# A transformer backbone in two layers on one core: the post-norm gates reach all partitions by transfers through DRAM, and layer 1's conditioning adds up in four strips

## The reference, cut to what matters

```python
def ada_params(cvec, w, b):                       # w: (1024, 6 * 1024)
    return jnp.split(jax.nn.silu(cvec) @ w + b, 6, axis=-1)

def pre_mod(x, g, shift, scale):
    return rms_norm(x, g) * (1 + scale) + shift

def post_add(x, y, g, gate):
    return x + gate * rms_norm(y, g)

for l in range(DEPTH):                            # DEPTH = 2
    need_ctx = l < DEPTH - 1
    sh1, sc1, g1, sh2, sc2, g2 = [m[:, None, :] for m in ada_params(c, ada_w[l], ada_b[l])]
    csh1, csc1, cg1, csh2, csc2, cg2 = ada_params(c_ctx, ada_w[l], ada_b[l])
    ...
    x = post_add(x, y, mix_post_g[l], g1)
    f = conv_ffn(pre_mod(x, ffn_pre_g[l], sh2, sc2), ffn_w_up[l], ffn_conv_w[l], ffn_conv_b[l], ffn_w_down[l])
    x = post_add(x, f, ffn_post_g[l], g2)
    if need_ctx:
        ...                                       # the same for xc with cg1, csh2, csc2, cg2
```

## Time and profile before

| | |
|---|---|
| runs of the kernel before | median 1597.65 us (1597.47 to 1603.56, three runs) |
| the profiled execution | 1596.83 us, of it 1595.0 us span from the first to the last instruction |
| PE busy | 1487.5 us, 93% |
| DVE, ACT, POOL busy | 966.3, 722.4, 596.5 us |
| granted TensorE clock, mean | 0.979 of full speed |

### The profile page before, as it was taken

One profiled execution on the slowest core, in us unless ns is written; L12 is line 12 of the kernel. 1 busy time (PEld: TensorE's weight loads), 2 busy tenths in 40 slices (PEclk: granted clock), 3 DMA queues, 4 the chain that ended last, 5 costly groups with the idle time before them and its releaser, 6 DMA issues.

```text
span 1595.0 us, 22240 instructions
## 1 busy us (share of the span) xinstructions
PE 1487.5 (93%) x7628; PEld 1202.1 (75%) x7628; DVE 966.3 (61%) x1476; ACT 722.4 (45%) x1242; POOL 596.5 (37%) x529
## 2 busy tenths in 40 slices
PE   4988898999999999999999698899999999999997
PEld 1877467787888888887888576677777888888886
DVE  2457687557687668743334575788885544444455
ACT  2332476544332333223353545487775544444453
POOL 2351354242222222322333531375552344443454
PEclk8999899999999999999999899999999999999999
DMA  8230850112464346311222111110002233332232
GB/s 336 56 98 1 293 184 1 53 59 87 145 184 117 109 145 184 105 40 53 63 65 66 48 53 55 52 53 1 1 1 81 78 93 94 103 92 67 92 95 103
DMA packets 128122, 143.89 MB, mean 90 GB/s; under 512 B 7164, under 2 KB 95488, under 8 KB 127024
## 3 DMA queue, kind: packets, MB, share of 16 engines
q1 hardware_dynamic: 128048, 142.91, 28.6%
HBM read 140.79 MB, written 2.10 MB: 90 GB/s over the span
## 4 chain that ended last, share of the span: by engine, by line
PE 82%; DVE 7%; ACT 3%; DMA 3%; POOL 2%; issue 2%; SPq 0%; DVEq 0%; POOLq 0%; ACTq 0%
PE ps L470 23%; PE ps L471 22%; PE ps L472 22%; PE ps L1427 4%; PE ps L1413 3%; PE ps L1438 2%; DMA start_w<-in_ada_w_dram 2%; PE ps L1440 2%; DMA ada_w<-in_ada_w_dram 1%; PE ps L2075 1%; PE ps L1330 1%; POOL w_lo L462 1%; PE ps L924 1%; DVE hT_lo L803 1%; ACT prob L1467 1%
## 5 line engine op out<-in xcount | busy, mean ns | idle before, releaser
L462 POOL TENSOR_TENSOR w_lo<-raw,w_hi 128x1024 fp32r<-128x1024 f32 (+1 forms) x183 | 346.9, 1898 | 627.5 <-ACT w_hi L455 627.5
L470 PE MATMUL ps<-hT_hi,w_hi 128*128 128x512 f32 (+1 forms) x1096 | 387.5, 354 | 9.3 <-DVE hT_lo L803 5.0
L471 PE MATMUL ps<-hT_lo,w_hi 128*128 128x512 f32 (+1 forms) x1096 | 384.8, 351 | 0.0
L472 PE MATMUL ps<-hT_hi,w_lo 128*128 128x512 f32 (+1 forms) x1096 | 382.6, 349 | 0.0
L455 ACT ACTIVATE w_hi<-raw 128x1024 fp32r<-128x1024 f32 (+1 forms) x200 | 172.9, 866 | 197.0 <-PE ps L472 166.2
L470 PEld LDWEIGHTS ps<-hT_hi,w_hi 128*128 128x128 f32 x1096 | 207.1, 189 | 47.1 <-DVE hT_lo L803 6.0
L472 PEld LDWEIGHTS ps<-hT_hi,w_lo 128*128 128x128 f32 x1096 | 206.5, 188 | 28.8
L471 PEld LDWEIGHTS ps<-hT_lo,w_hi 128*128 128x128 f32 x1096 | 207.1, 189 | 26.9
L2301 DVE TENSOR_TENSOR g_lo<-act_g,g_hi 128x768 fp32r<-128x768 f32 (+1 forms) x82 | 104.2, 1277 | 155.9 <-ACT g_hi L2256 155.5
L470 PE MATMUL ps<-w_hi,g_hi 128*128 128x512 f32 x410 | 160.4, 391 | 3.5 <-DVE g_lo L2301 3.0
L472 PE MATMUL ps<-w_hi,g_lo 128*128 128x512 f32 x410 | 159.6, 389 | 0.0
(11 more groups left out here) (247 smaller groups left out, 2500.7 us busy)
## 6 DMA issues: line engine op xcount, KB each, us to landing
raw<-in_ffn_w_up_dram SPq DMA_DIRECT2D x84, 512.0 KB, 3.9
ada_w_up<-in_ada_w_dram SPq DMA_DIRECT2D x48, 512.0 KB, 4.2
raw<-in_ffn_w_down_dram SPq DMA_DIRECT2D x84, 256.0 KB, 2.6
ada_w<-in_ada_w_dram SPq DMA_DIRECT2D x32, 512.0 KB, 5.2
start_w<-in_ada_w_dram SPq DMA_DIRECT2D x8, 1024.0 KB, 11.4
raw<-in_c_w_qkv_dram SPq DMA_DIRECT2D x12, 512.0 KB, 3.7
raw<-in_ab_w_in_dram SPq DMA_DIRECT2D x8, 512.0 KB, 4.8
raw<-in_ab_w_out_dram SPq DMA_DIRECT2D x8, 512.0 KB, 4.3
```

The lines of the kernel that those rows point to most:

```text
L462: by.tensor_tensor(w_lo[:, slot, 0:width], raw[:, n % RAW, 0:width], w_hi[:, slot, 0:width].bitcast(F32), ALU.subtract).then_inc(lo_split, 1)
L470: nc.tensor.matmul(outp, s_hi, m_hi, start=first, stop=False, skip_group_check=True)
L471: nc.tensor.matmul(outp, s_hi, m_lo, start=False, stop=False, skip_group_check=True)
L472: return nc.tensor.matmul(outp, s_lo, m_hi, start=False, stop=last, skip_group_check=True)
```

## The change

The gate products and their copies go. SP writes the finished gate rows to an internal DRAM tensor once per layer (`gate_out`), and reads each gate back as one row to 128 partitions (`gate_in`), at the end of the out loads (layer 0), behind the fourth out load (layer 1), and at the end of the up loads (both layers). Layer 1's conditioning has other rows: stream v, half h of the columns at partition 64 v + 32 h, all in bank 6; so the sums have four strips, and bias, transposes, columns and gate gains follow in pieces of 512 columns.

```diff
-        select_v = keep("select_v", [P, 2, 32])
+        select_v = keep("select_v", [P, 32])
...
+        ada1_rows = beside_up[0][:, 0, 0:BANK]
...
-            return 96 + 2 * (5 - i) + v if l else 2 * i + v if i < 2 else 32 + 2 * (i - 2) + v
+            return 64 * v + 5 - i if l else 32 + 2 * (i - 2) + v
...
-        def ada_turn(pe, n, b):
+        def ada_rows_turn(pe, n, b):
 
             pe.wait_ge(s("ada_biased"), n)
-            for k in range(KC):
-                mm = nc.tensor.transpose(bank(b, 2 * BANK)[:, k * P:(k + 1) * P], gate_rows[:, k * P:(k + 1) * P],
-                                         ident[:, :])
+            for c in range(4):
+                mm = nc.tensor.transpose(bank(b)[:, c * P:(c + 1) * P], gate_rows[:, c * P:(c + 1) * P], ident[:, :])
             mm.then_inc(s("ada_turned"), 1)
...
+        def ada1_bias(dve):
+
+            dve.wait_ge(s("ada_rows_landed"), 16 * (2 + ADA1_SMALL))
+            for v in range(2):
+                for half in range(2):
+                    rows = slice(64 * v + 32 * half, 64 * v + 32 * half + 6)
+                    op = nc.vector.tensor_tensor(gate_rows[rows, 0:BANK], ada1_rows[rows, :], beside_up[2][rows, 0:BANK],
+                                                 ALU.add)
+            op.then_inc(s("ada_biased"), 1)
...
+        gate_copy = (nc.dram_tensor("gate_copy0", (8, D), F32, kind="Internal").ap(),
+                     nc.dram_tensor("gate_copy1", (2, D), F32, kind="Internal").ap())
+        GATE_COPIES = (1, 3)
+
+        def gate_out(sp, l):
+
+            sp.wait_ge(s(f"gates_made{l}"), 1)
+            if l == 0:
+                sp.dma_start(gate_copy[0][:, :], gate_rows[ADA0_ROW:ADA0_ROW + 8, :]).then_inc(s("gates_out"), 16)
+            else:
+                for sub in range(2):
+                    r = ada_row(1, (2, 5)[sub], 0)
+                    sp.dma_start(gate_copy[1][sub, :].rearrange("(h n) -> h n", n=BANK), gate_rows[r:r + 33:32, 0:BANK]
+                                 ).then_inc(s("gates_out"), 16)
+
+        def gate_in(sp, l, sub):
+
+            sp.wait_ge(s("gates_out"), 16 * GATE_COPIES[l])
+            for v in range(1 if l else 2):
+                row = sub if l else 6 * sub + v
+                sp.dma_start(gate[:, v, :], gate_copy[l][row, :].partition_broadcast(P)
+                             ).then_inc(s(f"{('mixpost', 'ffnpost')[sub]}{l}_gate"), 16)
...
-            dve.wait_ge(s(f"{tag}_gate"), 2 * (2 if nt == ALL_T else 1))
+            dve.wait_ge(s(f"{tag}_gate"), 16 * (2 if nt == ALL_T else 1))
...
+                if l == 1 and m == 3:
+                    sp.wait_ge(s("qk_steps1"), rope_plan(1)[0][-1])
+                    gate_in(sp, 1, 0)
+            if l == 0:
+                gate_out(sp, 0)
+                sp.wait_ge(s("mixpost0_acc"), ALL_T)
+                gate_in(sp, 0, 0)
...
-                    if l == 1 and n == 0 and k == 1:
-                        gates()
                     for j in TURN_BEHIND[l].get(k, ()) if last else ():
                         if j == 0:
-                            pe.wait_ge(s(f"{tag}_gate"), 4 if nt == ALL_T else 2)
+                            pe.wait_ge(s(f"o_read{l}"), 2 * len(groups))
+                            pe.wait_ge(s(f"o_sum{l}"), 2 * len(groups))
+                            pe.wait_ge(s(f"{tag}_ysq"), OUT_DONE[l])
                         mid_turn(pe, l, j)
-                if l == 0 and n == 1:
-                    gates()
...
+            if l == 0:
+                sp.wait_ge(s("ada_mac"), (TURNS - 1) * (2 * KC) + START_MACS)
+            else:
+                sp.wait_ge(s("mixpost1_post"), post_count(LAT_T, LAT_T - 1, 3, "mixpost1"))
+            gate_in(sp, l, 1)
...
             if l == 0:
-                for half in range(2):
-                    nc.tensor.matmul(ps[96:128, 6 + half, :], select[:, 0:32],
+                for r in range(0, P, 32):
+                    nc.tensor.matmul(ps[r:r + 32, 6, :], select[:, 0:32],
...
                 for v in range(ada_streams):
                     for half in range(2):
-                        mm = nc.tensor.matmul(ps[96:128, 6 + half, :], select_v[:, v, :],
+                        r = 64 * v + 32 * half
+                        mm = nc.tensor.matmul(ps[r:r + 32, 6, :], select_v[:, :],
                                               beside_up[0][:, v, half * BANK:(half + 1) * BANK],
                                               start=False, stop=True, skip_group_check=True)
...
-            gate_tensor(pe, l, tag, 1, (0, 1))
-
...
-                if half == 0 and nt == ALL_T:
-                    gate_tensor(pe, l, tag, 1, (2, 3))
                 if l == 0 and half == 1:
-                    pe.wait_ge(s(f"{tag}_gate"), 4)
-                    ada_turn(pe, 2, 6)
+                    ada_rows_turn(pe, 2, 6)
...
                 if l == 0:
+                    gate_out(sp, 1)
```

More of the change, by code:

```diff
@@ new lines, in ada1_columns @@
+        def ada1_columns(dve):
+            dve.wait_ge(s("ada_turned"), 2)
+            turned = bank(6).rearrange("p (c r) -> p r c", r=P)
+            for sub, v in ((0, 0), (0, 1), (1, 0)):
+                for half in range(2):
+                    kk = slice(4 * half, 4 * half + 4)
+                    r = 32 * half + ada_row(1, 3 * sub, v)
+                    g = 16 * sub + 8 + 4 * half
+                    nc.vector.tensor_copy(add_col[:, sub, v, kk], turned[:, r, :])
+                    nc.vector.scalar_tensor_tensor(out=mul_col[:, sub, v, kk], in0=turned[:, r - 1, :], scalar=1.0,
+                                                   in1=cols[:, g:g + 4], op0=ALU.add, op1=ALU.mult)
+            for half in range(2):
+                rows = slice(32 * half, 32 * half + 6)
+                op = nc.vector.tensor_tensor(gate_rows[rows, 0:BANK], gate_rows[rows, 0:BANK], beside_up[3][rows, 0:BANK],
+                                             ALU.mult)
+            op.then_inc(s("gates_made1"), 1)
@@ L700, in start_tensor @@
                         norm_turn(pe, "mix0", k)
-            pe.wait_ge(s("ada_biased"), 1)
-            for c in range(4):
-                mm = nc.tensor.transpose(bank(START_TURNED)[:, c * P:(c + 1) * P], gate_rows[:, c * P:(c + 1) * P],
-                                         ident[:, :])
-            mm.then_inc(s("ada_turned"), 1)
+            ada_rows_turn(pe, 1, START_TURNED)
             close(pe, "pe")
@@ L1765, in out_tensor @@
             batches = out_batches(l, nt)
-            def gates():
-                pe.wait_ge(s(f"o_read{l}"), 2 * len(groups))
-                pe.wait_ge(s(f"o_sum{l}"), 2 * len(groups))
-                pe.wait_ge(s(f"{tag}_ysq"), OUT_DONE[l])
-                gate_tensor(pe, l, tag, 0, range(4 if nt == ALL_T else 2))
             for n, batch in enumerate(batches):
@@ L1913, in out_scalar @@
             else:
-                gate_scalar(act, tag, range(2))
                 second_half(0)
```

85 lines of the change are left out of this document (22 added, 63 removed).

## The result

The changed kernel took 1578.8 us (median of 4 runs, 1576.78 to 1582.88) against 1597.56 us for the kernel before on the same chip, ratio 0.988 with an interval of 0.986 to 0.991: 14.7 to 22.4 us off. The forecast was 1579.2 us, 18.4 us off.

A forecast was written before the change was run, and what follows sets the result against it. The prediction took TensorE (PE), busy 93% of the span, as the bound. Gates 8.5 us plus strips and related 9.9 us made 18.4 us off 1597.65, giving 1579.2 us; range 1573 to 1589.

The forecast's parts named there:

- The gate products: Out and down projections of both layers: gate products leaving PE save 3.91 + 1.72 + 1.72 + 0.6 + 0.55 = 8.5 us.
- the inner pair: Layer 0's down, after its first three units: two gate products leave PE and their 1.72 us comes back whole.
- (d): Rival: granted clock falls to half at other moments, 1 to 2 us either way; only widens the range, no chance given.
- the sum: Whole kernel: gates 8.5 plus strips and related 9.9 give 18.4 us off, 1579.2 us; forecast as summed has 78%.
- the starts: Start of each down: unit 1 waits for g_lo anyway, so 0.6 and 0.55 us saved, not 1.98 each.
- The strips: Layer 1's conditioning in the up projection: sums save 5.1 and 3.6, zero product 0.8; with 0.4 from transposes, 9.9 us.
- What is added: Gate transfers on SP's queue and smaller DVE operations: price 0, bounded by 2 us; layer 0's out gates land near 314.
- The margin: Layer 0's out: gates landing at 314 against a need by about 317.4, 3.4 us to spare, 0.7 slack on top.
- a landing at 11.4 us: Layer 0's out: if the gate reads took 11.4 us, they would land at 319.3 and cost about 1.5 us.
- (a): Rival, layer 1's conditioning: strips do not overlap, 9.5 us of sums and zero products stay, 1588.7 us; 7%.
- (b): Rival: PE less free, chains over DVE, ACT, POOL end last in out projections, up meets DVE; half kept, 1588; 9%.
- (c): Rival, layer 0's out: one-row broadcast uses few engines; with one, 53.5 us transfer, gate 46 us late, 1625 us; 3%.

The follow-up runs named there:

- the two halves: Against the kernel before, each half of the change alone: gates by transfers only, 1587.76 us, ratio 0.9926; conditioning in four strips only, 1592.4 us, ratio 0.9952.

## Why the prediction was right

**What bounds the kernel.** That PE is the bound, and that what leaves it comes back, held: 9.3 us in a stage where PE was busy 344.89 of 345.

**The gate products.** 3.91 us in layer 0's out: 3.90 from the last product with `ow_ada` to the transposes, in both executions of the changed kernel. Over the whole stage it is 3.9 in the kernel with only the transfers, 3.5 in the changed one and 1.9 in its other execution; these losses lie ahead of the place where the products stood, and in the last case the granted clock was 0.91 in the 20 us before it (288 to 308). 1.72 us in the inner pair: shown by putting it back, 1.7. 1.72 in layer 1's out: 1.7 in one execution, 0.2 in the other, whose granted clock over the stage is 0.94 for 0.97. That isn't rare: of the eight executions with gates by transfers three have 59.2 us there with the clock at 0.94, and five 57.7 to 58.0 at 0.97, while none of the six with gates by products has 0.94. So in three of eight the clock took this term back, which rival (d) allowed for either way and the sum did not. 0.6 and 0.55 at the starts: 0.57 and 0.45, with the wait seen, and seen to go when products fill it. This was the step on which 2.8 us hung, between the slots and the distances, and the distances were right.

**The strips.** 9.5 us predicted in the up projection, 9.3 measured; the difference is the 0.98 of two strips for the 0.92 assumed, four times. The wrong step was to take half of a pair, 1.83 / 2, for the time of one product and so for the bound from below: a product alone takes 0.97. The Trainium skill's rule for a pack of column tiles (TensorE: Matmul & The Clock Gate, Measured speedup vs the span model) is one product's duration plus 4 ns for each further tile. With the 0.97 it gives, as an estimate, some 0.98 for two and for four, and the rows show 0.98 and 0.99. The rule holds here to 0.01 us, and the 0.90 to 0.92 that the prediction worked out from it had the wrong duration put in.

**What is added.** Price 0, and nothing was paid: PE never waited for a gate. The landing at 6.1 us behind the release (the sixth first-half tile done) was met (5.8 from the issue, which follows it at once). The margin was mis-sized, 3.4 us with 0.7 on top for 5.6: my reckoning amounts to 20.9 us from the first use to the transposes (339.0, which is 342.94 less 3.91, minus 318.1), the runs show 19.7, and the gates came 0.3 us sooner than I had them: 4.1 + 1.2 + 0.3 = 5.6. As I read the rows, the last tiles follow one another on DVE faster than on PE when the chain is pressed, which a reckoning back from one tile doesn't see; that reading wasn't tested by itself. The statement that a landing at 11.4 us costs 1.5 us was wrong with it; 5 us late cost nothing.

**The rivals.** (a) and (b) are excluded by the two halves. (c) was a fair rival with a good price: over one engine the gates come 36.4 us later than they do, 5.6 are covered, and PE waits 30.55. It was 11 us too dear in the transfer, since one engine moved 1.04 MB in 42.2 us, 24.7 GB/s with the issue and the landing in it, and not at the 19.6 that I had from the mean of the whole queue. (d) was sized too small for a single execution: the way to layer 0's attention alone, which no edit touches, takes from 230.3 to 236.0 us in the changed kernel.

**The sum.** By the stages that the change touches it is 3.5 + 9.3 + 2.6 + 1.7 + 0.3 = 17.4 us in the changed kernel's first profile, for 18.4. By the medians it is 18.8 and 22.9. The difference is layer 1's projection, 1.3 to 5.3 us shorter, of which 0.9 us goes with the faster load, part with the clock, and the rest has no shown cause, less 0.4 to 1.5 us that layer 1's attention gives back, and the way to layer 0's attention, which spreads over 3.7 us in three executions of the kernel before and 5.7 in two of the changed one. So 1579.2 was close to the first median partly by luck, because two small misses of opposite sign met: about 1 us too much for the touched stages, and a gain outside them that the prediction didn't have.

## What to carry to other kernels

Price a removed instruction by the distance to the next thing that must wait anyway, and not by its slot: the same pair of products was worth 1.72 us inside a stage and 0.5 at its start. Small sums that write one strip of the array belong side by side in one bank; beyond the first strip they are nearly free. Don't take half of a pair for the time of one: a row of one alone was in the trace. A broadcast through DRAM takes some 5 us for 512 KB, 5.8 to the first use for two of them, and apart from SP's issues no engine's time, so put it where its first use is that far behind its release, and read all 128 partitions in one transfer: split as 127 and 1, two of them took 42.2 us.

## What the runs showed of the hardware that I had not expected

One, two and four fp32 products in strips of their own cost the same, 0.97, 0.98 and 0.99 us, for 1.83 and 3.55 of two and four in one strip. A transfer over one engine ran at 24.7 GB/s and held the issuing queue: SP's four issues took 27.11 us, and the weight loads behind them waited. A load of one size in one place takes 3.6 or 4.9 us until it is used, the same within 0.1 us in the three executions of before and in the two of the changed kernel, and different between kernels, by a cause that I didn't find. And a wait of 5.25 us on PE cost 6.8 us in all: over the 8 us from 345.00 on, the wait's last 0.4 and what follows, the granted clock was 0.70, more than half of them at the lower of its two levels, 1.2 GHz.
